# A hybrid decoder step on eight cores: state-space table loads move to ScalarE's queue, and filler matmuls go

## The reference

```
h = RMSNorm(x);  z = h @ W_in          # columns: zb | zc | zv | zu | ga | gs
ya = zb * conv3_causal(zc * zv)         # 512 channels
ys = S5(zu)                             # 32 groups of 16 channels, 64 complex states each
ys = g * sigmoid(g @ w_glu + b_glu),  g = gelu(ys)
m  = sigmoid(ga) * (ya @ Wb[:512]) + sigmoid(gs) * (ys @ Wb[512:])
x  = x + m @ W_out
x  = x + (silu(h2 @ Wg) * (h2 @ Wu)) @ Wd,   h2 = RMSNorm(x)   # inner width 2816
```

## Time and profile before

| | |
|---|---|
| profiled execution, device time | 3782.45 us |
| its span, first to last instruction of the slowest core | 3780.9 us |
| spans of the eight cores | 3762.2 to 3780.9 us |
| mean granted TensorE clock, by core | 0.982 to 0.986 of full speed |
| PE busy | 3626.7 us (96%), 24514 matmuls |
| DVE busy | 1807.1 us (48%) |
| ACT busy | 1086.7 us (29%) |
| POOL busy | 327.7 us (9%) |
| HBM traffic | 574.40 MB read, 56.12 MB written |

### The profile page before, as it was taken

One profiled execution on the slowest core, in us unless ns is written; L12 is line 12 of the kernel. 1 busy time (PEld: TensorE's weight loads), 2 busy tenths in 40 slices (PEclk: granted clock), 3 DMA queues, 4 the chain that ended last, 5 costly groups with the idle time before them and its releaser, 6 DMA issues.

```text
span 3780.9 us, 68910 instructions; the slowest of 8 cores (3762.2 to 3780.9 us)
## 1 busy us (share of the span) xinstructions
PE 3626.7 (96%) x24514; PEld 2042.4 (54%) x24514; DVE 1807.1 (48%) x3557; ACT 1086.7 (29%) x2073; POOL 327.7 (9%) x550
## 2 busy tenths in 40 slices
PE   7899999999999999899998999989999999989998
PEld 3356666666666666566664444444444444444443
DVE  4866566565664756544225342245313542254323
ACT  3134214342134421343123321132203431033212
POOL 1100111001110011100000000000000000000000
PEclk8999999999999999999999999999999999999999
DMA  7264458544584445854437544484435644465443
GB/s 137 76 155 79 75 108 186 99 80 83 114 192 90 74 93 116 193 108 92 76 65 189 112 72 77 68 177 81 76 70 111 146 78 73 70 135 84 71 78 84
DMA packets 253499, 391.58 MB, mean 104 GB/s; under 512 B 157808, under 2 KB 180976, under 8 KB 247024
## 3 DMA queue, kind: packets, MB, share of 16 engines
q0 software_dynamic: 67968, 243.30, 38.9%
q1 hardware_dynamic: 185200, 143.87, 13.4%
HBM read 574.40 MB, written 56.12 MB: 167 GB/s over the span
## 4 chain that ended last, share of the span: by engine, by line
PE 89%; DMA 6%; issue 2%; DVE 2%; ACT 1%; SPq 0%; DVEq 0%; ACTq 0%
PE ps L684 82%; PE ps L1330 2%; DMA dy<-YY 2%; PE ps L717 1%; DMA TAB<-stash 1%; DMA X<-xT 1%; PE ps L1108 1%; DMA R<-stash 1%; DVE SC L580 1%; DMA du<-R 1%; PE ps L941 1%; PE ps L1081 0%; PE ps L1034 0%; DMA UU<-du 0%; PE ps L928 0%
## 5 line engine op out<-in xcount | busy, mean ns | idle before, releaser
L684 PE MATMUL ps<-H,RING 128*128 128x512 bf16 (+2 forms) x12160 | 2177.0, 339 | 8.7 <-ACT YY L1115 3.0
L684 PEld LDWEIGHTS ps<-H,RING 128*128 128x128 bf16 x12160 | 1188.5, 98 | 942.3 <-issue 24.6
L684 PE MATMUL ps<-R,RING 128*128 128x384 bf16 (+2 forms) x6400 | 1163.0, 338 | 9.0 <-DVE X L1246 4.0
L684 PEld LDWEIGHTS ps<-R,RING 128*128 128x128 bf16 x6400 | 624.6, 98 | 501.3 <-issue 14.3
L1266 DVE TENSOR_TENSOR R<-SC,ps 128x384 bf16<-128x384 f32 (+2 forms) x440 | 256.2, 583 | 727.6 <-PE ps L684 714.3
L1265 ACT ACTIVATE SC<-ps 128x384 f32<-128x384 f32 (+2 forms) x440 | 226.1, 514 | 1218.0 <-PE ps L684 1120.3
L672 POOL DMA_DIRECT2D RING<-wpk x472 | 250.6, 532 | 3247.2 <-PE ps L684 3042.3
L1246 DVE TENSOR_TENSOR X<-X,ps 128x384 f32<-128x384 f32 (+2 forms) x480 | 270.2, 582 | 407.5 <-PE ps L684 406.0
L715 ACT ACTIVATE H<-X 128x384 bf16<-128x384 f32 (+2 forms) x304 | 156.6, 540 | 217.8 <-DVE X L1246 181.2
L739 DVE SCALAR_TENSOR_TENSOR H<-X,PRM,SC 128x384 bf16<-128x384 f32 (+2 forms) x304 | 171.5, 637 | 68.7 <-DMA SC<-s0in 33.6
L580 DVE TENSOR_TENSOR SC<-TB 128x512 f32<-128x512 f32 x256 | 178.1, 723 | 5.6
(11 more groups left out here) (164 smaller groups left out, 1649.5 us busy)
## 6 DMA issues: line engine op xcount, KB each, us to landing
RING<-wpk POOLq DMA_DIRECT2D x440, 512.0 KB, 7.0
TAB<-stash SPq DMA_DIRECT2D x24, 1792.0 KB, 10.6
stash<-TAB SPq DMA_DIRECT2D x16, 1792.0 KB, 7.0
R<-stash SPq DMA_DIRECT2D x8, 1792.0 KB, 14.9
RING<-wpk POOLq DMA_DIRECT2D x32, 384.0 KB, 5.9
du<-R SPq DMA_DIRECT2D x32, 256.0 KB, 11.4
UU<-du SPq DMA_DIRECT2D x32, 256.0 KB, 4.7
dy<-YY SPq DMA_DIRECT2D x32, 256.0 KB, 7.1
```

The source lines that it names most:

```text
L684: subs.append((lambda e, u=u, kw=kw, c=c, src=src, i=i: e.matmul(ps[:, 0:blk.n], lhsT=u.ap(kw, c), rhs=src(blk), start=(i == 0), stop=(i = ...
```

## The change

The 32 table loads of `ssm_f` (24 into TAB, 8 into R) are issued by ScalarE instead of SP, with four semaphores of their own. The planner's part that puts in matmuls on constants is removed, with the four lines that set it up. The planner's model of transfers is replaced: each issuing engine has a queue time of its own, a transfer takes 1 + 0.7 times the number of other queues that are then busy as long, and the fixed parts become 0.7 and 1.4 us. As the list of each engine comes from that simulation, the order on all of them can change.

```diff
-    NSEM = {"sp": 14, "pool": 8}
+    NSEM = {"sp": 14, "pool": 8, "act": 4}
...
-        o.dur = 0.9 if eng == "pool" else 0.06
+        o.dur = {"pool": 0.9, "sp": 0.06, "act": 0.1}[eng]
...
-        bus = 0.0
-        dcount = {"sp": 0, "pool": 0}
+        qfree = {e: 0.0 for e in self.NSEM}
+        dcount = {e: 0 for e in self.NSEM}
...
-                if e == "pe" and npe > 0 and all(d.done and d.end < t for d in self.idle_deps) and (not f or f[0][0] > t + 0.3) and len(self.idle_pool.free) > 1 and ndummy < 20000:
-                    p = self.idle_pool
-                    slot = p.free.pop(0)
...
-                    o.dur = 0.22
...
-                    self.order[e].append(o)
...
-                beg = max(bus, t + dur + 0.6)
-                bus = beg + o.nbytes / self.DBW
-                o.end = bus + 1.3
+                beg = max(qfree[e], t + dur + 0.7)
+                share = 1 + 0.7 * sum(1 for e2 in qfree if e2 != e and qfree[e2] > beg + 0.3)
+                qfree[e] = beg + o.nbytes * share / self.DBW
+                o.end = qfree[e] + 1.4
...
-            S.dma("sp", lambda e, f=f, tab=tab: e.dma_start(out=tab[:, 0:TW], in_=stash[l, f]), [("ST", l, f)], tkk, 128 * TW * 4)
+            S.dma("act", lambda e, f=f, tab=tab: e.dma_start(out=tab[:, 0:TW], in_=stash[l, f]), [("ST", l, f)], tkk, 128 * TW * 4)
...
-    S.idle_fn = lambda e, b: e.matmul(PSUM[b][:, 0:512], lhsT=ONESB[:], rhs=bc(IDB[:, 0:128], [[0, 4], [1, 128]]), start=True, stop=True)
```

More of the change, by code:

```diff
@@ L202, in schedule @@
         nleft = len(ops)
-        npe = sum(1 for o in ops if o.eng == "pe")
-        ndummy = 0
         pos = {e: 0 for e in self.ENGS}
@@ L283, in schedule @@
                     push(f[0][0], e)
-                if e == "pe" and npe > 0 and all(d.done and d.end < t for d in self.idle_deps) and (not f or f[0][0] > t + 0.3) and len(self.idle_pool.free) > 1 and ndummy < 20000:
-                    p = self.idle_pool
-                    slot = p.free.pop(0)
[L287 to L291, removed]
-                    o.dur = 0.22
[L293 to L303, removed]
-                    self.order[e].append(o)
-                    p.last[slot] = (o,)
-                    push(o.end, (p, slot))
-                    push(o.end, e)
                 continue
             o = pick
-            if e == "pe":
-                npe -= 1
             dur = o.dur
@@ L1326, in build @@
           [("CVS", l, f) for l in range(DEPTH) for f in range(4)], [], 128 * 128)
-    S.idle_pool = PP
-    S.idle_mode = FULL
-    S.idle_deps = (S.lastw[C_("IDB")], S.lastw[C_("ONESB")])
-    S.idle_fn = lambda e, b: e.matmul(PSUM[b][:, 0:512], lhsT=ONESB[:], rhs=bc(IDB[:, 0:128], [[0, 4], [1, 128]]), start=True, stop=True)
     S.schedule()
```

## The result

The changed kernel takes 3824.77 us (median of 4 runs, from 3821.41) beside 3781.68 for the kernel before: ratio 1.0112, interval 1.0092 to 1.0132. The forecast was 3743, so the sign is wrong and the time lies above the range. The profiled execution took 3827.14 us, its span 3825.6.

A forecast was written before the change was run, and what follows sets the result against it. TensorE's projection, 82% of the chain of waits, was taken as the bound. Terms -20 - 15 - 10 + 0 + 4 + 3 = -38 us took the profiled 3782.45 to 3744, hence 3743 us for the median; range 3680 to 3800.

The forecast's parts named there:

- Bounces no longer behind tables: Second half's three stages: layout bounces land sooner off the tables' queue and the plan improves; -20 us.
- the first half: Three stages: the late table itself cannot be shortened, only bounces behind it and the plan improve; -10 us.
- the change of halves: Between halves: output stores go past the table, ending VectorE's wait for a store's buffer; -15 us.
- three signs of being wrong: du<-R above 10 us; ScalarE idle over 2 us a load; the stretch 91 to 270 us growing over 8 us.
- Nothing gained: Rival: shared DMA engines leave bounces beside tables as slow as behind; clock and issue cancel small gains; 3782, chance 0.14.
- ScalarE stands (slower, 3815): Rival: table loads heading ScalarE's stream wait for their tile and hold up evictions; +35 us, chance 0.19.
- Constant matmuls: 602 fewer PE instructions, but the awaited data comes no sooner; booked 0, lower bound -11 us.
- Clock: PE's granted clock falls without constant matmuls, mostly hidden by VectorE during table building; two falls exposed, +4 us.
- Issue from ScalarE: 32 table loads take ScalarE's time, on the path only in the stages, about a quarter; +3 us.

The follow-up runs named there:

- d_only: Kernel before with its order unchanged, the 602 constant matmuls planned but not emitted; ratio 0.9952, profiled 3754.01 us.
- after_sp: Changed kernel with the table loads issued by SP again, replanned; ratio 1.0019, profiled 3781.00 us.
- after_order_sp: Changed kernel's own order kept, the 32 table loads moved from ScalarE's list to SP's at their planned time; ratio 1.0065, profiled 3804.83 us.

## Why the prediction was wrong

**The step that failed** is the first term, "Bounces no longer behind tables", in its sentence that the new planner's charge is "nearer to the earlier trace rows than before; so L1016 moves behind the L993s and filler goes where PE would wait". The charge of 0.9 to 1.7 us times its share, plus 2.1, was 3 to 5 us for a bounce. Measured are 8.4 and 9.3 in the median and 15.9 to 16.8 for the du<-R that stands on the chain in each first-half stage. I had compared the charge with R<-dy and UU<-du, whose medians are 4.3 and 4.7 us, and not with a bounce beside a table. What I concluded for this term, that a bounce no longer has to wait for the table's last packet, no run bears out. The plan of the old bus, which made bounces wait for tables, served the chip better: against it the new order costs 43 us with the loads on SP, and 57 with them on ScalarE (1.0112 against 0.9960). I took -20, -10 for the first half and -15 for the change of halves; the stretches, which hold all terms together, came out at +8.5, +28.0 and +4.5. None of the three signs of being wrong that I had named came up (du<-R above 10 us, ScalarE standing over 2 us a load, the start growing by over 8 us: 8.4, 0.27 a load, and 4.7 up to the first steady stretch); none of them looked at the plan.

**"Nothing gained"** had the right mechanism, and I gave it 0.14. A bounce beside a table is about as slow as behind it (15.91 and 16.01 us against 13.04 and 11.18 on the chain, in one order). The Trainium skill, "DMA: Bandwidth & Descriptors", section "Issuing engines are not separate DMA queues", says that more issuing engines save only the time to start transfers; the runs of the old order agree (0.9960 against 0.9952), those at 170 GB/s, which differ in their plans too, less so (13 us). What that rival lacked was the price: it let the plan stay as it was. A planner that believes in a gain which isn't there moves work, and the waits that this makes are the loss.

**"ScalarE stands (slower, 3815)"** came nearest in time, but not by its mechanism: the chain gives ScalarE's queue 0%, its waits for tables fell from 58.8 to 32.5 us, and its pauses before its 32 loads are 8.6 us in sum, 0.27 each, the longest 1.96, where the rival needed over 1.2 each. The longest:

```profile
2033.22 0.43 ACT L688 ACTIVATE R<-X 128x272 bf16<-128x272 f32 x1 [0.58 <-DVE X L1219]
2035.61 0.33 ACTq L988 DMA_DIRECT2D R<-stash  x1
```

About 18 us do go when the loads leave ScalarE in this order, but 14 of them where the small transfer dys<-YY lands late beside a table.

**Constant matmuls**, booked at 0 with -11 as the bound, measured 0 in the order of after (1.0112 against 1.0113), -18 in the old order and -55 in the plan at 170 GB/s. So the term was right for the change as made; its bound was wrong for the other two plans, because I looked for a gain in VectorE's idle time alone. In the earlier trace rows L1330 had 2% of the chain, which is work on the path; a matmul that fills an idle moment is in the way when the awaited data comes. The first small matmul of the first stage starts at 194.1 us before and 187.4 in d_only, and 29 us of the chain of before between 118 and 200 us are constant matmuls, such as these:

```profile
133.12 3.90 PE ps L1330 x18
```

**Clock**, booked at +4: the fall came where it was foreseen; its price by itself no run shows. From 91 to 200 us, after:

```profile
91.00:200.00 109.00, 26.88 (x282) 18.04 (x283) 98.30 (x182) 20.19 (x37) 21.99 (x17) 0.54 0.27 95
```

Against the earlier trace rows the clock fell from 0.95 to 0.54, near the 1.2 GHz level, and VectorE's 98.30 us hid it: d_only, with 0.55 there, has its largest gain in this very part (-12.6).

**Issue from ScalarE**, +3: a load takes 0.33 us there, and the old order lost about 3 us by it, which its interval does not tell from nothing.

## What to carry to other kernels

When a change gives a list scheduler a new model of a resource, predict the plan as well as the resource: check each duration that the model will believe against the landings measured in the company in which the transfer flies, not against the kind's best. A belief that is too early makes waits on the path (42.1 and 92.5 us here), one that is too late costs as well (3.6% at 130 GB/s), and one constant deserves a sweep whenever the model around it changes. Filler matmuls that keep a clock up belong only where nothing on the path can come free behind them: here they cost 0, 18 or 55 us by the plan around them.

## What the runs showed that was not expected

A transfer can hold the engine that issues it for long. After, a transfer of 8 KB held SP for 11.06 us and stands on the chain with 15.71:

```profile
211.85 11.06 SPq L1157 DMA_DIRECT2D scv<-CIN  x1
```
```profile
211.85 15.71 DMA scv<-CIN
```

At 170 GB/s the same transfer takes 17.41 us on the chain. The queue of the tables does not decide it: before, with the tables on SP itself, what SP issued at this place was a table load, and that was held:

```profile
210.38 8.90 SPq L1015 DMA_DIRECT2D TAB<-stash  x1
```

In after_sp it is 10.19 us for the table load, in after_order_sp 8.09 for the 8 KB. What fills the queue there was not tried. And 55 us for 782 matmuls that the plan puts only into moments it believes idle is more than a quarter of their busy time of 202.3.
